# Attention stage of a hybrid decoder step: where the next queries and the gate tiles' low parts are cut

## The reference, cut to what matters

```python
s_w = jnp.einsum('nthgd,nshd->nthgs', q, kv_win[:, :, 0]) * scale
p_w = masked_softmax(s_w, w_mask[None, :, None, None, :])
o_w = jnp.einsum('nthgs,nshd->nthgd', p_w.astype(q.dtype), kv_win[:, :, 1])
...
return gates[..., 0:1] * o_c + gates[..., 1:2] * o_s + gates[..., 2:3] * o_w
...
q, kv_c, kv_s, kv_w, g_nsa, u, g_merge = jnp.split(z, cuts, axis=-1)
```

## Time and profile before

| | us |
|---|---|
| median of 3 runs | 1895.89 (1894.03 to 1898.45) |
| the profiled execution's own time | 1901.07 |
| its span, from first to last instruction | 1899.3 |
| stage of the change in the trace | about 360 to 842 |

### The profile page before, as it was taken

How to read it: one execution, slowest core, us unless ns; L and a number is a source line. 1 busy time by engine, 2 the same in 40 slices (tenths; PEclk the granted TensorE clock), 3 DMA queues, 4 the chain that set the end, 5 groups by cost and what they waited for, 6 DMA issues and landing times. The chain is left out here.

```text
span 1899.3 us, 25887 instructions
## 1 busy us (share of the span) xinstructions
PE 1758.0 (93%) x10828; PEld 1628.7 (86%) x10828; DVE 717.9 (38%) x1376; ACT 600.0 (32%) x1106; POOL 447.5 (24%) x269
## 2 busy tenths in 40 slices
PE   6899996889999999887999898999999999999997
PEld 2799985778778778765999898999999999999996
DVE  2411115545666777652445463211211121112135
ACT  3322123334455556441334353201221122012311
POOL 1545441111101001000134472221222222212411
PEclk9899996899999999995999999999999999999998
DMA  9334425221110101022642031111111111111421
GB/s 290 89 100 126 107 81 170 64 60 36 40 42 27 33 28 31 23 60 65 196 139 67 34 124 45 48 53 45 45 46 45 45 45 46 45 45 47 132 67 57
DMA packets 205768, 137.14 MB, mean 72 GB/s; under 512 B 44629, under 2 KB 201473, under 8 KB 205609
## 3 DMA queue, kind: packets, MB, share of 16 engines
q1 hardware_dynamic: 195755, 123.06, 22.5%
q10 hardware_dynamic: 9894, 12.39, 2.0%
HBM read 115.82 MB, written 21.92 MB: 73 GB/s over the span
## 5 line engine op out<-in xcount | busy, mean ns | idle before, releaser
L2099 POOL TENSOR_TENSOR ff_lo<-ff_raw,ff_hi 128x1024 fp32r<-128x1024 f32 x56 | 137.0, 2449 | 490.0 <-ACT ff_hi L1915 490.0
L1223 PE MATMUL gate_ps<-h_hi,gate_w_cut 128*128 128x344 f32 x768 | 229.8, 347 | 13.6 <-ACT gate_sum L1344 13.4
L1223 PEld LDWEIGHTS gate_ps<-h_hi,gate_w_cut 128*128 128x128 f32 x768 | 143.3, 195 | 19.4 <-ACT gate_sum L1344 12.3
L2276 PE MATMUL ff_acc<-h_hi,ff_hi 128*128 128x344 f32 x672 | 142.6, 321 | 0.6 <-DVE relu_c L2425 0.6
L2276 PE MATMUL ff_acc<-h_lo,ff_hi 128*128 128x344 f32 x672 | 142.6, 320 | 0.0
L2276 PE MATMUL ff_acc<-h_hi,ff_lo 128*128 128x344 f32 x672 | 141.9, 319 | 0.0
L1317 ACT ACTIVATE prob<-scores,bias 128x640 f32<-128x640 f32 (+7 forms) x192 | 106.1, 558 | 108.0 <-DVE bias L1390 62.9
L746 POOL TENSOR_TENSOR gate_w_cut<-gate_w_raw,gate_w_cut 128x1024 fp32r<-128x1024 f32 x16 | 38.6, 2412 | 403.1 <-ACT gate_w_cut L741 403.1
L2276 PE MATMUL ff_acc<-f_hi,ff_hi 128*128 128x344 f32 x576 | 124.1, 324 | 7.1 <-issue 7.1
L1915 ACT ACTIVATE ff_hi<-ff_raw 128x1024 fp32r<-128x1024 f32 x56 | 58.7, 1052 | 226.3 <-DMA ff_raw<-in_w_ff_dram 226.3
L1417 DVE TENSOR_TENSOR p_lo<-pT,p_hi 128x512 fp32r<-128x512 f32 (+1 forms) x148 | 101.4, 686 | 66.5 <-ACT p_hi L1328 65.8
(11 more groups left out here) (375 smaller groups left out, 3960.4 us busy)
## 6 DMA issues: line engine op xcount, KB each, us to landing
ff_raw<-in_w_ff_dram SPq DMA_DIRECT2D x56, 512.0 KB, 4.0
wa_rest<-in_w_ada_dram SPq DMA_DIRECT2D x16, 1024.0 KB, 5.2
gate_spill<-gate_sum SPq DMA_DIRECT2D x48, 172.0 KB, 1.8
gates<-gate_spill SPq DMA_DIRECT2D x16, 516.0 KB, 4.8
wa<-in_w_ada_dram SPq DMA_DIRECT2D x8, 1024.0 KB, 9.4
gate_w_raw<-in_w_in_dram SPq DMA_DIRECT2D x16, 512.0 KB, 4.2
w_raw<-in_w_in_dram SPq DMA_DIRECT2D x30, 256.0 KB, 6.3
xt<-in_x_prompt_dram ACTq DMA_DIRECT2D x4, 1024.0 KB, 9.4
```

The source lines that it names most:

```text
L1223: last = pe.matmul(gps[:, 0:CH], gw_cut[:, 1 - u % 2, a, k], h[:, k, c * CH:(c + 1) * CH], start=(k == 0 and n == 0), stop=(k == KD - 1 an ...
L2099: pool.tensor_tensor(lo, raw, hi.bitcast(F32), ALU.subtract).then_inc(wflo_ready, 1)
L2276: last = pe.matmul(accs[s][:, c, 0:CH], w[:, z % SLOTS, k], x[:, k, c * CH:(c + 1) * CH], start=(k == 0 and n == 0), stop=(k == KD - 1 and ...
```

## The change

The queries of block i+1 are cut for one key head at a time, at the last block of unit (i, kv, window), on ScalarE and VectorE; TensorE waits for each head by itself. GpSimd's loop is gone. VectorE makes the low parts: tile 1 whole, ahead of block 0; of the others in one, two or four pieces, at the ends of the blocks after the one with the high cut (tiles 2 and 3, which are used in the very next block, whole at the end of that same block; tile 4 whole; tiles 5 to 7 in two pieces; tiles 8 to 15 in four).

```diff
-        def split_q_hi(act, i):
-
-            for kv in range(KVH):
-                act.activation(qd[rows_of(kv), kv], qT[rows_of(kv), :, i * P:(i + 1) * P], ACT.Copy, scale=SCALE).then_inc(qhi_ready, 1)
...
+        def split_q_hi(act, i, kv):
+
+            act.activation(qd[rows_of(kv), kv], qT[rows_of(kv), :, i * P:(i + 1) * P], ACT.Copy, scale=SCALE).then_inc(qhi_ready, 1)
+
+        def split_q_lo(dve, i, kv):
+
+            own, other = rows_of(kv), rows_of(1 - kv)
+            dve.wait_ge(qhi_ready, KVH * i + kv + 1)
+            dve.tensor_copy(qd[other, kv], qd[own, kv].bitcast(F32))
+            dve.scalar_tensor_tensor(ql[own, kv], qT[own, :, i * P:(i + 1) * P], SCALE, qd[own, kv].bitcast(F32),
+                                     ALU.mult, ALU.subtract).then_inc(qlo_ready, 1)
...
+        block_of_step = {x: t for t, xs in enumerate(steps_at) for x in xs}
+        gate_rests = {}
+        for t in range(NBL):
+            for u in gate_cuts_at(t):
+                room = block_of_step[12 * u] - t - 1
+                parts = 4 if room >= 4 else 2 if room >= 2 else 1
+                for part in range(parts):
+                    gate_rests.setdefault(t + min(room, part + 1), []).append((u, part, parts))
...
-                        if k == 0 and kv == 0 and not sel:
-                            pe.wait_ge(qlo_ready, i + 1)
+                        if k == 0 and not sel:
+                            pe.wait_ge(qlo_ready, KVH * i + kv + 1)
...
-                    def cut_q(i):
-                        act.wait_ge(scores_done, GRP * 2 * KVH * i)
-                        split_q_hi(act, i)
+                    def cut_q(i, kv):
+                        act.wait_ge(scores_done, GRP * (2 * KVH * (i - 1) + 2 * kv + 2))
+                        split_q_hi(act, i, kv)
...
-                            i, kv, sel = units[n]
-                            if k == GRP - 1 and kv == KVH - 1 and sel and i + 1 < NB:
-                                cut_q(i + 1)
+                        i, kv, sel = units[blocks[t][0]]
+                        if last_block(t) and not sel and i + 1 < NB:
+                            cut_q(i + 1, kv)
...
-                @block.gpsimd
-                def _(pool):
-                    for u in range(1, NGT):
-                        cut_gate_lo(pool, u)
...
+                    def gate_rest(u, part, parts):
+
+                        k, z = slice(part * KD // parts, (part + 1) * KD // parts), 1 - u % 2
+                        dve.wait_ge(gw_hi_ready, u + 1)
+                        last = dve.tensor_tensor(gw_cut[:, z, GLO, k], gw_raw[:, z, GLO, k], gw_cut[:, z, GHI, k].bitcast(F32), ALU.subtract)
+                        if part == parts - 1:
+                            last.then_inc(gw_lo_ready, 1)
...
                     shares(0, 1)
+                    gate_rest(1, 0, 1)
...
-                        for n, k in jobs_at(t):
-                            i, kv, sel = units[n]
-                            if k == GRP - 1 and kv == KVH - 1 and sel and i + 1 < NB:
-                                split_q_lo(dve, i + 1)
+                        i, kv, sel = units[blocks[t][0]]
+                        if last_block(t) and not sel and i + 1 < NB:
+                            split_q_lo(dve, i + 1, kv)
+                        for u, part, parts in gate_rests_at(t):
+                            gate_rest(u, part, parts)
```

More of the change, by code:

```diff
@@ L704, in hybrid_step @@
         qhi_ready, qlo_ready, zeroed_q = sem("qhi_ready"), sem("qlo_ready"), sem("q_lo_zeroed")
-        def split_q_hi(act, i):
-            for kv in range(KVH):
-                act.activation(qd[rows_of(kv), kv], qT[rows_of(kv), :, i * P:(i + 1) * P], ACT.Copy, scale=SCALE).then_inc(qhi_ready, 1)
-        def split_q_lo(dve, i):
-            dve.wait_ge(qhi_ready, KVH * (i + 1))
-            for kv in range(KVH):
-                own, other = rows_of(kv), rows_of(1 - kv)
-                dve.tensor_copy(qd[other, kv], qd[own, kv].bitcast(F32))
-                last = dve.scalar_tensor_tensor(ql[own, kv], qT[own, :, i * P:(i + 1) * P], SCALE, qd[own, kv].bitcast(F32),
-                                                ALU.mult, ALU.subtract)
-            last.then_inc(qlo_ready, 1)
+        def split_q_hi(act, i, kv):
[6 more added lines that the diff above has]
+                                     ALU.mult, ALU.subtract).then_inc(qlo_ready, 1)
         at = buf.slabs(3, scratch3)
@@ L900, in _ @@
                     act.activation(crows[:], cps[:], ACT.Copy).then_inc(crows_ready, 1)
-                    split_q_hi(act, 0)
+                    for kv in range(KVH):
+                        split_q_hi(act, 0, kv)
                     take_mix(2)
@@ L1091, in _ @@
                     dve.wait_ge(zeroed_q, 1)
-                    split_q_lo(dve, 0)
+                    for kv in range(KVH):
+                        split_q_lo(dve, 0, kv)
                     dve.wait_ge(kchi_ready, 1)
@@ L1157, in gate_cuts_at, with gate_rests_at @@
             return [x // 12 + 1 for x in steps_at[t] if x % 12 == 5 and 2 <= x // 12 + 1 < NGT]
+        block_of_step = {x: t for t, xs in enumerate(steps_at) for x in xs}
[6 more added lines that the diff above has]
+                    gate_rests.setdefault(t + min(room, part + 1), []).append((u, part, parts))
+        def gate_rests_at(t):
+            return gate_rests.get(t, [])
         cs = buf.slabs(3, scratch3)("cs", [P, NS, NPG, 2 * P])
```

## The result

| | before | after |
|---|---|---|
| median of the runs | 1897.17 us (1894.03 to 1900.74, 4 runs) | 1876.09 us (1875.52 to 1877.76, 4 runs) |
| ratio, 95% interval | | 0.9901 [0.9877, 0.9924] |
| profiled execution / its span | 1901.07 / 1899.3 | 1876.33 / 1874.5 |
| stage, from 360 us to the last stored gate sum | 482 | 458 |

The change gains 21.1 us on the medians and 24.7 between the profiled executions. 24 us of that are the stage; what follows it takes 1056.9 us before and 1056.6 after.

A forecast was written before the change was run, and what follows sets the result against it. TensorE, busy 93% of the span, was taken as the bound, so only its idle time or lower clock could pay. Terms -30.7 - 5.5 + 4.6 + 1.0 + 4.6 + 3.4 = -22.6 us gave 1873, range 1856 to 1889.

The forecast's parts named there:

- the wait for gate tiles: TensorE waiting for a gate tile's low part: put at nothing, and named as a sign of being wrong.
- the holds: VectorE held by GpSimd at 395, 420, 645, 680 and 795: removal gains 5.5 us, between 2 and 10.7.
- all six stretches: Stretches from 455, 510, 570, 630, 695, 760 with the double split: 13.6 us idle plus 17.15 clock, 30.7 us won.
- The half-splits: One-head splits at the ends of window units, 14 times: cost 4.6 us, bounds 0 and 15.5.
- one clock stretch: One more stretch at the lower clock, from idle time the first units keep: cost 3.4 us.
- The gate tiles on VectorE: Low parts made on VectorE: tile 1 ahead of the second unit's maxima 1.0 us, the later tiles 4.6 us.
- the quarter share: Of 18.5 us of later gate-tile work on VectorE, a quarter reaches the end: 4.6 us, between 0 and 18.5.
- Tiles 2 and 3, 1.0 us each: At 395 and 420, 2.2 us of hold goes and 1.23 us of VectorE work comes: 2.0 us gained together.
- Rival 1: Split's idle time goes but TensorE's clock does not come back: -8.8 us, 1887; chance 0.17.
- rival 3: VectorE becomes the bound, every piece ahead of work TensorE wants: +16 us, 1912; chance 0.06.
- Rival 4: The split's wait moves to the new place; holds and additions remain, within 4 us; chance 0.06.
- Rival 2: Nearly all idle time and clock of the eleven stretches comes back, additions hidden: -39.6 us, 1856; chance 0.17.

The follow-up runs named there:

- e12: Kernel before, double split kept, GpSimd subtracting only an eighth of the columns of tiles 2 to 15, nothing added on VectorE: 1877.29 us, ratio 0.99.
- e3: Kernel after without any query split after block 0, all blocks using block 0's queries: 1868.0 us, ratio 0.9852.
- e2: Kernel after with the old double split, so only the gate tiles' part of the change: 1883.86 us, ratio 0.9933.
- e4: Kernel after with an unread maximum over the same columns ahead of each half or quarter piece on VectorE (38 instructions, 17.2 us): 1894.94 us, ratio 0.9987.
- e8: Kernel after with tile 1 back on GpSimd and quarters only where six blocks are left: 1876.47 us, ratio 0.9911.
- e9: Kernel after with pieces of tiles 5 to 15 and whole tiles 1 and 3 on GpSimd, block 3's queries cut one unit later: 1865.12 us, ratio 0.982.
- e10: Kernel before, double split kept, tiles 5 to 15 in pieces on GpSimd, tiles 1 to 4 whole on VectorE: 1881.15 us, ratio 0.9906.

## Why the prediction was right, and where its working was wrong

The forecast was −22.6 us on the profiled execution and 1873 on the median; it came to −24.7 and 1876.09. What was to be seen was seen: idle time 25.2 where about 25 was named, mean clock 0.98, casts of 0.42, a stage 24 us shorter, the rest unchanged. One of its signs of being wrong was seen as well, the wait for gate tiles. The total is right, but the working behind it is not: 30.7 us were booked to the split where at most 16.4 are found, and 8.0 to the holds where 20.5 are found. That these two errors cancel is only partly luck: the places were counted once, and since the change takes both causes away, what is booked to the wrong one still goes. It is luck that the rest cancels too, the smaller terms below.

- **"I take all six stretches as won, idle and clock: 30.7 us"** is the step that failed. The double split itself was worth at most 16.4 us there (e12), of which 2.8 stay in the kernel after. In the three early places GpSimd's instruction fell on VectorE's work too: it held a cast of the split for 2.2 us in two of them (2.61 for 0.42 at 510, and the like at 457) and a multiply for 1.3 in the third. I booked the whole of these places to the split, although the same rows are named among the holds a paragraph later. Without the holds they lose none of their 10.25 us of clock (e12). The place at 630, which has no GpSimd, was typical of the late ones alone.
- **The holds: 5.5 us, "between 2 and 10.7"**, or 8.0 before the 1.23 us of work each of tiles 2 and 3. Measured: 20.5 (e12). I priced them by the idle time at the five places that were not the split's, and so missed the three inside the six places and the clock lost with them. The upper bound was wrong for the same reason.
- **The half-splits, 4.6, and one clock stretch, 3.4**: 8.0 together. e3's medians give 8.1, but the agreement is luck: its traced execution wins 3.3 us in the stage and 4.5 behind it. The idle time and the clock that the half-splits cost are for the most part one event, at 480.
- **The gate tiles on VectorE**: tile 1's 1.0, tiles 2 and 3 with 2.5 and the quarter share with 4.6 make 8.1; from e12 to e2 it is 6.6 to 8.8. "A quarter" was about right for the amount, and wrong as a rule (e4).
- **"TensorE's wait for a tile's low part: ... so nothing"** was wrong by 2.2 us of waits, for tiles 8 and 9. The last quarter comes at the end of the block before the use, with no block between. Mending it gained no time (e8).
- **Tiles 2 and 3, 1.0 us each**: at 395 1.88 us of idle became 0.80, at 420 3.49 became 2.55. Right.
- **Rival 1**, the clock does not come back, fell (22.2 us lost became 8.0), and so did rival 3, though with 17 us more of VectorE's time and twice the single delay e4 gives back nearly the whole gain. Rival 4 fell by the wait for `p_lo`, 12.7 us before and 2.7 after. **Rival 2** took 39.6 us to be the most that there was to win; e9 reaches 30.8.

What stays open: why nearly equal idle time at one place goes with different losses of clock (last section), and with it the last 2 or 3 us of every price above. Open too is how much of the holds' price lies in the length of GpSimd's instructions and how much in the place where they fell.

## What to carry to other kernels

Where two causes meet in one stretch, its idle time and its clock must not be given to the one that the change names: look which stretches have only one of them, and price the other from a kernel that has it alone. A helper engine that shares a port did harm here by the length of one instruction and by where it fell, not by its busy share: most of the same work in pieces, released beside work that takes one of its inputs from PSUM, cost 4 to 6 us instead of 20 (e10 against e12, tiles 2 to 4 on VectorE included). And an engine with a third of its time idle is not free to take any work: 22 us in mostly short pieces cost 6.6 to 8.8, and 17 us more, right beside those pieces, cost in full.

## What the runs showed of the hardware that was not expected

- The same wait, followed by different clocks: at 420 TensorE stands 2.55 us in the kernel after and the stretch of 10 us has a clock of 0.83; in e8 it stands 2.53 us and the clock is 0.66. At 500 to 515 it stands 2.01 us in several waits in the kernel after and loses none.
- In the traced executions idle times of separate edits nearly add up, lost clock does not. Idle: split −5.8, gate part −4.4, both −11.4. Clock: −5.5, −14.0, both −14.2.
- GpSimd's subtraction in quarters takes 0.751 us each, 3.0 for a tile where the whole takes 2.41; VectorE's takes 0.416 and 1.219.
